# A ring of split projection weights placed 64 bytes lower in a one-core hybrid decoder block

## The chip, the cores and the metric

The kernel runs on one NeuronCore of one Trainium2 chip. The metric is the device time of one execution in microseconds (us); a lower time is better. The clock of TensorE (PE in the profile) has two levels in these records, 1.2 and 2.4 GHz, and the profile gives the granted share of the upper one.

## What is computed

One decoder layer on 16 meta tokens and 512 real tokens, width 2048: an RMS norm, one wide input projection, a gated DeltaNet branch, a pooling branch, a gated merge with an output projection, and a SwiGLU feed-forward part. Cut to what matters here:

```python
h = concatenate([meta, x], axis=1)                 # 528 tokens
hn = rms_norm(h, norm_mix_w)
proj = hn @ w_in                                   # q, k, v, z, beta/decay logits, p, gate_a, gate_b
q, k, v = silu(causal_dwconv(qkv)); q, k l2-normed
o = gated_delta_rule_chunked(q, k, v, beta, g)     # 8 heads of 128
y_a = (rms(o) * silu(z)) @ w_proj_a
y_b = (pool(p) @ pool_w * pool_scale) @ w_proj_b
h += (sigmoid(gate_a) * y_a + sigmoid(gate_b) * y_b) @ w_out
h += (silu(rms_norm(h) @ w_gate) * (rms_norm(h) @ w_up)) @ w_down
out = rms_norm(h)[:, 16:]
```

All products keep close to float32: both operands are split into a high part (rounded to fp32r) and a low part (the remainder), and three products are summed: high by high, high by low, low by high.

## The kernel before, in words

**Stages, in order of time.** The weights `w_in` are read in chunks of 128x1024 floats (512 KB); four chunks make a unit of 256 output channels, and a chunk holds four of the 16 blocks of 128 input channels (`kt = c + 4*k` for chunk `c` of the unit and `k` from 0 to 3). Each chunk lands in `w_raw` by a DMA of SP, ScalarE (ACT) rounds it into `w_hi` (line 935), VectorE (DVE) subtracts and writes `w_lo` (line 1378), and TensorE multiplies. `w_raw`, `w_hi` and `w_lo` have four slots each; chunk `c` of every unit uses slot `c`.

- First unit (`first_unit`, line 2105): one unit of q/k/v; all its products with tokens 0 to 255 (moving operand 256 wide), then all with tokens 256 to 527 (272 wide).
- Stage A (line 2128, `chunk_products`): 11 more units of q/k/v. The moving operand comes from `hn_halves`: for each stationary block a product 256 wide and one 272 wide, so 11 x 4 x 2 x 4 x 3 = 1056 such pairs.
- Stage G (2128 again): 16 units for the gates, interleaved with the DeltaNet recurrence's small matmuls; the moving operand is `hn_real`, all 512 real tokens at once: 16 x 96 = 1536 matmuls.
- Stage P: 4 units for the pooling input, `hn_halves`: 384 pairs.
- Stage Z: 4 units for z, `hn_real`: 384 matmuls of 512.
- Merge (2128, tiles `w_hi_m`, `w_lo_m`), then the output projection (2432 to 2434), the feed-forward gate and up products (2457 to 2459, 44 units of 7 x 24 = 168 matmuls 256 wide) and the down projection (2432 to 2434 again, 512 wide).

The order of TensorE's work is written out by hand and the same before and after. Before a chunk TensorE waits for `lo_ready` (the count of DVE's low parts); ACT waits for `chunk_used` before it writes a slot again.

**Where the tiles lie.** What the change touches is addresses. All begin as offsets in bytes within a partition, and the code asserts that `whi_at`, `wlo_at`, `mixer_consts_at`, `hn_at` and `ext_at` are the same modulo `BEAT` = 256; call that place 0. Worked out from there:

- `w_hi` slot `c` begins at 64 + 4160*c from `whi_at`. As 4160 = 16*256 + 64, its place modulo 256 is 64*(c+1). A stationary block inside begins at a multiple of 512 further on, so it has the place of its slot. `w_lo` is laid out alike. `w_hi_m` and `w_lo_m` (merge) have no gaps: place 0.
- `hn_hi[:, kt, :]` and `hn_lo[:, kt, :]` have rows of 528 floats = 2112 = 8*256 + 64 bytes. With `kt = c + 4*k`, row `kt` has place 64*c. `hn_halves` begins at its column 0 or 256: place 64*c. `hn_real` begins at column 16, 64 bytes on: place 64*(c+1).
- Merge and down projection: both operands at place 0.
- Feed-forward: the moving tiles `s_hi`, `s_lo` are at `hn_at + 64`, place 64; the stationary tiles `hi_a`, `lo_a`, `hi_b`, `lo_b`, `hi_c`, `lo_c` at place 0. One stationary pair differs from unit to unit: `hi_2_0`, `lo_2_0` (place 0) serve units 4 to 43, `hi_2_1`, `lo_2_1` (place 64) serve units 0 to 3; the program's names for both in the trace are `hi` and `lo`, used in the third product (S2) of each unit.

```python
def two(tiles, n):
    return tiles[1] if isinstance(n, int) and n < STEADY else tiles[0]
```

Of the kernel before, what the change touches and what calls it, by code (L numbers as in the profile page):

```python
# [140 lines left out]
def hybrid_block(nc, x, meta_tokens, norm_mix_w, w_in, conv_w, a_log, dt_bias, o_norm_w, w_proj_a, pool_w,  # L141
                 pool_scale, w_proj_b, w_out, norm_ffn_w, w_ffn_gate, w_ffn_up, w_ffn_down, norm_final_w, out):
    ctx = ExitStack()
    with ctx:
# [14 lines left out]
        def place(name, shape, dtype=F32, at=None):  # L159
            size = int(np.prod(shape[1:])) * 4  # L160
            offset = top[0] if at is None else at
            if at is None:
                top[0] += (size + 63) // 64 * 64
            return nc.alloc_sbuf_tensor_at(name, shape, dtype, offset=offset)
# [5 lines left out]
        def ring(name, step, first):  # L170
            return [place(f"{name}{i}", [P, CHUNK], F32R, at=top[0] + first + (4 * CHUNK + step) * i) for i in range(SLOTS)]

        LINE = 64
        whi_at = top[0]
        whi, whi_m = ring("w_hi", LINE, LINE), ring("w_hi_m", 0, 0)
        top[0] += SLOTS * (4 * CHUNK + LINE)
        wlo_at = top[0]
        wlo, wlo_m = ring("w_lo", LINE, LINE), ring("w_lo_m", 0, 0)
        top[0] += SLOTS * (4 * CHUNK + LINE)

        minus_half = place("minus_half", [P, 16])
# [2335 lines left out]
```

## Time and profile before

| | |
|---|---|
| median of 3 runs | 2654.39 us (2654.24 to 2655.65) |
| the profiled execution | 2655.96 us, its span 2654.2 us |
| mean granted TensorE clock | 0.993 |
| busy: PE, PE weight load, DVE, ACT, POOL | 98%, 89%, 68%, 38%, 12% |
| HBM | 151 GB/s mean over the span |

The profile shows one execution. A matmul's duration in it is from its start to the end of its results, and successive matmuls overlap; what a matmul costs in a stream is the distance from its start to the next one's. The timeline view prints starts to 0.01 us and merges neighbours that use the same tiles into one row ("x2").

### The profile page before, as it was taken

How to read it: one execution, taken by the hardware profiler on the slowest of the kernel's cores; microseconds unless marked ns; L12 is line 12 of the kernel's file. 1: busy time of each engine (PE TensorE's matmuls, PEld its weight loads, DVE VectorE, ACT ScalarE, POOL GpSimd, SP SyncE). 2: the span in 40 equal slices, each digit the busy share in tenths (PEclk: the TensorE clock that was granted, in tenths of full speed). 3: DMA queues.
4: the chain of work that ended last, by engine and by line, in shares of the span. 5: the costliest groups of instructions: out<-in, count | busy, mean ns of one | idle time of the engine just before them, and what ended most of it. 6: DMA issues, size and time to landing. Idle time of an engine off the chain costs nothing.

```text
span 2654.2 us, 43654 instructions
## 1 busy us (share of the span) xinstructions
PE 2604.5 (98%) x17278; PEld 2369.4 (89%) x17278; DVE 1816.0 (68%) x1714; ACT 999.0 (38%) x1016; POOL 318.9 (12%) x326
## 2 busy tenths in 40 slices
PE   7999999999999999999989999999999999999998
PEld 6999988888889977888879999999999998888886
DVE  5444555554543234558888888888888888888898
ACT  4443322222222232223454444444444444333334
POOL 6000034444431500100000000000000000000000
PEclk8999999999999999999999999999999999999999
DMA  4333333333333434689333444544454449866562
GB/s 145 98 87 95 84 87 88 91 83 91 88 90 92 110 87 165 231 282 324 127 138 124 161 155 148 173 153 156 147 179 150 154 150 344 279 198 218 161 203 102
DMA packets 346856, 400.84 MB, mean 151 GB/s; under 512 B 11626, under 2 KB 300563, under 8 KB 345619
## 3 DMA queue, kind: packets, MB, share of 16 engines
q1 hardware_dynamic: 287122, 335.39, 40.4%
q10 hardware_dynamic: 59664, 64.51, 7.1%
q8 instruction: 46, 0.75, 0.1%
q14 instruction: 24, 0.19, 0.0%
HBM read 328.02 MB, written 71.84 MB: 151 GB/s over the span
## 4 chain that ended last, share of the span: by engine, by line
PE 92%; DVE 3%; issue 1%; ACT 1%; DMA 1%; POOL 1%; SPq 0%; DVEq 0%; ACTq 0%; POOLq 0%
PE psum L2128 34%; PE psum L2457 10%; PE psum L2459 10%; PE psum L2458 10%; PE psum L2432 7%; PE psum L2433 6%; PE psum L2434 6%; PE psum L2286 2%; PE psum L2105 1%; PE psum L2297 1%; DMA w_raw<-in_w_proj_a 1%; PE psum L2372 1%; PE psum L2267 0%; DMA dn_raw<-in_w_ffn_down 0%; POOL hn_lo L766 0%
## 5 line engine op out<-in xcount | busy, mean ns | idle before, releaser
L2128 PE MATMUL psum<-hn_hi,w_hi 128*128 128x256 f32 (+1 forms) x1600 | 451.2, 331 | 0.0
L2128 PE MATMUL psum<-hn_lo,w_hi 128*128 128x256 f32 (+1 forms) x1600 | 450.0, 330 | 0.0
L2128 PE MATMUL psum<-hn_hi,w_lo 128*128 128x256 f32 (+1 forms) x1600 | 449.3, 330 | 0.0
L1378 DVE TENSOR_TENSOR w_lo<-w_raw,w_hi 128x1024 fp32r<-128x1024 f32 x144 | 190.1, 1321 | 260.7 <-ACT w_hi L935 259.7
L935 ACT ACTIVATE w_hi<-w_raw 128x1024 fp32r<-128x1024 f32 x144 | 152.2, 1058 | 415.8 <-PE psum L2128 387.6
L2128 PEld LDWEIGHTS psum<-hn_hi,w_hi 128*128 128x128 f32 x1600 | 271.0, 188 | 22.8 <-issue 0.2
L2128 PEld LDWEIGHTS psum<-hn_lo,w_hi 128*128 128x128 f32 x1600 | 270.8, 188 | 22.9 <-issue 0.7
L2128 PEld LDWEIGHTS psum<-hn_hi,w_lo 128*128 128x128 f32 x1600 | 270.5, 188 | 22.7
L2432 PE MATMUL psum<-dn_hi,act_hl 128*128 128x512 f32 x616 | 240.9, 391 | 2.0 <-DVE dn_lo L1712 2.0
L2434 PE MATMUL psum<-dn_hi,act_hl 128*128 128x512 f32 x616 | 240.3, 390 | 0.0
L2433 PE MATMUL psum<-dn_lo,act_hl 128*128 128x512 f32 x616 | 240.2, 390 | 0.0
L2457 PE MATMUL psum<-s_hi,hi_a 128*128 128x256 f32 x704 | 194.6, 276 | 1.0 <-DVE s_lo L1883 1.0
L2458 PE MATMUL psum<-s_lo,hi_a 128*128 128x256 f32 x704 | 194.4, 276 | 0.0
L2459 PE MATMUL psum<-s_hi,lo_a 128*128 128x256 f32 x704 | 194.4, 276 | 0.0
L2459 PE MATMUL psum<-s_hi,lo_b 128*128 128x256 f32 x704 | 194.4, 276 | 0.0
L2458 PE MATMUL psum<-s_lo,hi_c 128*128 128x256 f32 x704 | 194.4, 276 | 0.0
L2459 PE MATMUL psum<-s_hi,lo_c 128*128 128x256 f32 x704 | 194.4, 276 | 0.0
L2458 PE MATMUL psum<-s_lo,hi_b 128*128 128x256 f32 x704 | 194.4, 276 | 0.0
L2457 PE MATMUL psum<-s_hi,hi_c 128*128 128x256 f32 x704 | 194.4, 276 | 0.0
L2457 PE MATMUL psum<-s_hi,hi_b 128*128 128x256 f32 x704 | 194.4, 276 | 0.0
L920 POOL TENSOR_TENSOR rms<-rms_a,minus_half 128x1 f32<-128x1 f32 x4 | 2.6, 658 | 1281.9 <-DVE rms_a L2025 1281.9
L1185 ACT ACTIVATE hi<-t 128x1024 fp32r<-128x1024 f32 x44 | 46.8, 1064 | 267.9 <-DVE t L1829 267.9
(359 smaller groups left out, 6236.0 us busy)
## 6 DMA issues: line engine op xcount, KB each, us to landing
w_raw<-in_w_in SPq DMA_DIRECT2D x144, 512.0 KB, 3.9
ffn_raw<-in_w_ffn_gate SPq DMA_DIRECT2D x44, 1024.0 KB, 6.4
ffn_raw<-in_w_ffn_up SPq DMA_DIRECT2D x44, 1024.0 KB, 6.9
dn_raw<-in_w_ffn_down SPq DMA_DIRECT2D x32, 1024.0 KB, 8.3
act_hl<-act_dram SPq DMA_DIRECT2D x56, 512.0 KB, 9.1
act_dram<-comb_hi ACTq DMA_DIRECT2D x22, 896.0 KB, 4.2
act_dram<-comb_lo ACTq DMA_DIRECT2D x22, 896.0 KB, 6.2
out_raw<-in_w_out SPq DMA_DIRECT2D x16, 1024.0 KB, 10.9
```

The source lines that it names most:

```text
L935: act.activation(whi[s][:], raw[s][:], ACT.Copy).then_inc(S["hi_ready"], 1)
L1185: act.activation(two(hi_2s, n)[:], two(t2s, n)[:], ACT.Copy).then_inc(S["hi_ready"], 1)
L1378: dve.tensor_tensor(wlo[s][:], raw[s][:], whi[s][:].bitcast(F32), ALU.subtract).then_inc(S["lo_ready"], 1)
L2105: ins = pe.matmul(outs(m)[i], lhs, mv, start=kt == 0 and j == 0, stop=kt == KT - 1 and j == 2)
L2128: ins = pe.matmul(o, lhs, r, start=kt == 0 and i == 0, stop=kt == 4 * n_chunks - 1 and i == 2)
L2286: ins = pe.matmul(bank(1)[:, i, :], x[:, i, :], B[11][:, i, :], start=True, stop=True)
L2432: pe.matmul(out, a_hi, w_hi, start=start and i == 0, stop=False, skip_group_check=True)
L2433: pe.matmul(out, a_hi, w_lo, start=False, stop=False, skip_group_check=True)
L2434: ins = pe.matmul(out, a_lo, w_hi, start=False, skip_group_check=True, stop=i == k - 1 and (what in ("b21", "b22", "t4") or at_end and wha ...
L2457: pe.matmul(out, w_hi[:, k0 + k, :], s_hi[c][:, k, :], start=start and k == 0, stop=False, skip_group_check=True)
L2458: pe.matmul(out, w_hi[:, k0 + k, :], s_lo[c][:, k, :], start=False, stop=False, skip_group_check=True)
L2459: ins = pe.matmul(out, w_lo[:, k0 + k, :], s_hi[c][:, k, :], start=False, stop=stop and k == HEADS - 1, skip_group_check=True)
```

## The change

The two rings of the projection's weights lose their first 64 bytes; the distance between slots stays 4160, and `top` moves on by as much as before, so no other tile moves. The merge's tiles (`w_hi_m`, `w_lo_m`) stay.

```diff
         LINE = 64
         whi_at = top[0]
-        whi, whi_m = ring("w_hi", LINE, LINE), ring("w_hi_m", 0, 0)
+        whi, whi_m = ring("w_hi", LINE, 0), ring("w_hi_m", 0, 0)
         top[0] += SLOTS * (4 * CHUNK + LINE)
         wlo_at = top[0]
-        wlo, wlo_m = ring("w_lo", LINE, LINE), ring("w_lo_m", 0, 0)
+        wlo, wlo_m = ring("w_lo", LINE, 0), ring("w_lo_m", 0, 0)
         top[0] += SLOTS * (4 * CHUNK + LINE)
```

with

```python
def ring(name, step, first):
    return [place(f"{name}{i}", [P, CHUNK], F32R, at=top[0] + first + (4 * CHUNK + step) * i) for i in range(SLOTS)]
```

Slot `c` then has place 64*c. No instruction is added, removed or moved on any engine.

## Rows read from the trace of the kernel before

**Rows 1.** The page: the span, busy time and share of each engine.

```profile
span 2654.2 us, 43654 instructions
...
PE 2604.5 (98%) x17278; PEld 2369.4 (89%) x17278; DVE 1816.0 (68%) x1714; ACT 999.0 (38%) x1016; POOL 318.9 (12%) x326
```

**Rows 2.** The page: the chain that ended last, by engine.

```profile
PE 92%; DVE 3%; issue 1%; ACT 1%; DMA 1%; POOL 1%; SPq 0%; DVEq 0%; ACTq 0%; POOLq 0%
```

**Rows 3.** The view of waits, for PE: who it waited for, us, times, longest.

```profile
PE psum L2457 <- DVE s_lo L1907: 7.9, 1, 7.9
PE psum L2105 <- DVE w_lo L1378: 5.3, 3, 3.0
...
PE psum L2128 <- DVE gate_a L1769: 1.0, 1, 1.0
```

**Rows 4.** The groups by form: line 2128's matmuls, one of each width.

```profile
L2128 PE MATMUL psum<-hn_hi,w_hi 128*128 128x512 f32 x640 | 256.8, 401 | 0.0
...
L2128 PE MATMUL psum<-hn_hi,w_lo 128*128 128x272 f32 x480 | 138.4, 288 | 0.0
...
L2128 PE MATMUL psum<-hn_lo,w_hi 128*128 128x256 f32 x480 | 134.4, 280 | 0.0
```

**Rows 5.** Timeline of PE, stage A; each x2 is one pair.

```profile
266.59 0.40 PE L2128 MATMUL psum<-hn_hi,w_hi 128*128 128x256 f32 x2
266.83 0.40 PE L2128 MATMUL psum<-hn_lo,w_hi 128*128 128x256 f32 x2
...
268.03 0.40 PE L2128 MATMUL psum<-hn_hi,w_hi 128*128 128x256 f32 x2
```

**Rows 6.** Timeline of PE, feed-forward unit 3: S2 begins and ends.

```profile
1440.73 0.28 PE L2459 MATMUL psum<-s_hi,lo_a 128*128 128x256 f32 x1
...
1441.86 0.28 PE L2457 MATMUL psum<-s_hi,hi 128*128 128x256 f32 x1
...
1444.74 0.28 PE L2457 MATMUL psum<-s_hi,hi_b 128*128 128x256 f32 x1
```

**Rows 7.** Timeline of PE, unit 4: S2 begins and ends.

```profile
1461.06 0.28 PE L2457 MATMUL psum<-s_hi,hi 128*128 128x256 f32 x1
...
1463.78 0.28 PE L2457 MATMUL psum<-s_hi,hi_b 128*128 128x256 f32 x1
```

**Rows 8.** Timeline of PE, first unit, 256 wide alone: chunk 1's second half, chunk 3.

```profile
35.55 0.28 PE L2105 MATMUL psum<-hn_hi,w_hi 128*128 128x256 f32 x1
...
36.85 0.28 PE L2105 MATMUL psum<-hn_hi,w_lo 128*128 128x256 f32 x1
...
44.59 0.28 PE L2105 MATMUL psum<-hn_hi,w_hi 128*128 128x256 f32 x1
...
47.21 0.28 PE L2105 MATMUL psum<-hn_hi,w_lo 128*128 128x256 f32 x1
```

**Rows 9.** Timeline of PE, first unit, 272 wide alone: chunk 0 and chunk 1's start.

```profile
55.03 0.29 PE L2105 MATMUL psum<-hn_hi,w_hi 128*128 128x272 f32 x1
...
57.99 0.29 PE L2105 MATMUL psum<-hn_hi,w_hi 128*128 128x272 f32 x1
```

**Rows 10.** Timeline of PE, merge, 512 wide.

```profile
1119.96 0.39 PE L2128 MATMUL psum<-zb_hi,w_lo_m 128*128 128x512 f32 x1
...
1122.91 0.39 PE L2128 MATMUL psum<-zb_hi,w_hi_m 128*128 128x512 f32 x1
```

**Rows 11.** Timeline of PE, stage Z: first matmuls of two successive chunks, 24 apart.

```profile
921.58 0.39 PE L2128 MATMUL psum<-hn_hi,w_hi 128*128 128x512 f32 x1
...
927.06 0.39 PE L2128 MATMUL psum<-hn_hi,w_hi 128*128 128x512 f32 x1
```

**Rows 12.** Timeline of PE, feed-forward units 1 and 2: product A12 and S2.

```profile
1400.01 0.28 PE L2457 MATMUL psum<-s_hi,hi_a 128*128 128x256 f32 x1
...
1402.83 0.28 PE L2457 MATMUL psum<-s_hi,hi 128*128 128x256 f32 x1
...
1422.67 0.28 PE L2457 MATMUL psum<-s_hi,hi 128*128 128x256 f32 x1
```

**Rows 13.** The lines of the two splits: ns min/median/max, first and last start.

```profile
L1378 DVE TENSOR_TENSOR w_lo<-w_raw,w_hi x144: 1209/1225/2065, 25.5 to 985.5; 128x1024 fp32r<-128x1024 f32 x144
L1378 DVE TENSOR_TENSOR w_lo_m<-w_raw,w_hi_m x32: 1214/1225/1229, 1002.4 to 1178.7; 128x1024 fp32r<-128x1024 f32 x32
...
L935 ACT ACTIVATE w_hi<-w_raw x144: 1038/1059/1066, 23.7 to 984.4; 128x1024 fp32r<-128x1024 f32 x144
L935 ACT ACTIVATE w_hi_m<-w_raw x32: 1039/1047/1062, 1001.3 to 1177.6; 128x1024 fp32r<-128x1024 f32 x32
```

## The prediction

> **What bounds the kernel now.** I read the page first: PE is busy for 98% of the span [rows 1], and the chain that ended last runs over PE for 92% [rows 2]. The waits say the same from the other side: the longest single waits of PE are 7.9 and 5.3 us, and in the stages that use the rings (line 2128) it waited 1.0 us for one producer [rows 3]. So whatever changes the distance between two matmul starts in those stages lands in the time one for one, and nothing else in the change can. The change adds no instruction; it moves the stationary operand of line 2128 and line 2105 by 64 bytes against the moving one. What has to be priced is therefore a distance in ns, times a count. The counts are in the groups by form [rows 4]: three groups of 480 pairs (256 and 272 wide) make 1440 pairs in stages A and P, and three of 640 make 1920 matmuls 512 wide in stages G and Z.
>
> **What the spacing is now, and at which offset.** I call offset the place of the moving operand less that of the stationary one, modulo 256 bytes.
>
> - Stages A and P have offset -64. Six pairs start in 268.03 - 266.59 = 1.44 us, so a pair costs 240.0 ns [rows 5].
> - Merge has offset 0: 13 matmuls of 512 in 2.95 us, 226.9 ns each [rows 10]. I take this as the undisturbed rate. Scaled by width it is 113.5 ns for 256 columns and 120.6 for 272. The feed-forward part shows 113.3 for 256, below.
> - The feed-forward part has offset +64: in unit 4, 24 matmuls take 1463.78 - 1461.06 = 2.72 us, 113.3 ns each [rows 7].
>
> At the undisturbed rate a pair would take 113.3 + 120.4 = 233.7 ns (272/256 of 113.3 is 120.4), so today's pairs cost 6.3 ns more than that.
>
> **The row that speaks of alignment.** The kernel itself holds one trial of offset 0 at width 256. S2 of units 0 to 3 reads its stationary tile at place 64, where the moving tile is too; from unit 4 on the same product reads it at place 0. In unit 3, S2's 24 matmuls take 1444.74 - 1441.86 = 2.88 us, 120.0 ns each [rows 6], and the ten matmuls just ahead of it, at offset +64, took 1.13 us, 113 ns each [rows 6]. In unit 4 S2 has 113.3 ns [rows 7]. Nothing else differs between these places but 64 bytes of the stationary tile's address. So equal places cost 6.7 ns per matmul at width 256, and the address does matter. At width 512 equal places cost nothing in merge [rows 10]: a weight load of 128 columns has twice the time there, and I take it that this is why.
>
> The Trainium skill (TensorE: Matmul & The Clock Gate, step 1 of "What happens when you issue a matmul") says the opposite of the unit-3 row: PE has two independent SBUF read ports, so that loading the next weights doesn't take bandwidth from the running matmul. By that rule the move would change nothing, and 120.0 against 113.3 ns should not be there.
>
> **The change part by part.**
>
> 1. Stages A and P go from offset -64 to 0, 1440 pairs. For the 256-wide half the nearest row is S2 of unit 3: 120.0 ns. For the 272-wide half no row shows offset 0. Lower end: 120.4, its undisturbed rate, if the 16 further columns give the weight load the room it lacks; upper end: 120.4 + 6.7 = 127.1. Between them I take 123.5: in the first unit 272-wide matmuls run back to back and 24 of them take 57.99 - 55.03 = 2.96 us, 123.5 ns [rows 9]; that excess comes with the odd width, which the change doesn't touch. Sum: 243.5 ns for a pair, 3.5 ns more than now, x1440 = **+5.0 us**. The bounds of a pair are 240.4 (+0.6 us) and 247.1 (+10.2 us) if the S2 row carries over; and 233.7 (-9.1 us) if it does not.
> 2. First unit, offset -64 to 0. Alone, the 256-wide matmuls stand at 1.30 us for 11, 118 ns, in chunk 1, and at 2.62 us for 23, 114 ns, in chunk 3 [rows 8]. To 120.0 from between these is +4 ns on the some 60 that run at the full clock: **+0.3 us**. The second pass, 96 matmuls, stays as taken above; at most +3.6 ns x 96 = +0.3.
> 3. Stages G and Z go from offset 0 to +64, 1920 matmuls. A chunk in stage Z takes 927.06 - 921.58 = 5.48 us for 24, 228.3 ns [rows 11], against 226.9 undisturbed. Lower end: nothing is disturbed, -1.4 ns x 1920 = -2.7 us. Upper end: offset +64 isn't always clean; in unit 1 A12 takes 1402.83 - 1400.01 = 2.82 us for 24, 117.5 ns [rows 12], which is 4.2 over 113.3. Laid on the undisturbed 512-wide matmul that makes 231.1, +2.8 on today's 228.3, x1920 = +5.4 us. I take the middle, **+1.0 us** (rounded down, since the width gives room).
> 4. ACT's and DVE's splits write and read at moved addresses. Their medians in the ring's tiles are 1059 and 1225 ns, in the merge's tiles at place 0 1047 and 1225 ns [rows 13]: at most 12 ns in a thousand, and both engines have hundreds of us to spare there, so **0**. The cover is that PE is behind, not they: it waited for `w_lo` only in the first unit [rows 3].
> 5. The DMAs write `w_raw`, which doesn't move: **0**.
>
> Sum: +5.0 + 0.3 + 1.0 = **+6.3 us**. Against the profiled execution (2655.96 us, its span 2654.2 and 1.8 around it) that is 2662.3; that execution was 1.6 us above the median, so on the median of 2654.39 it is **2660.7 us**. A measurement of this kernel tells 0.2%, 5.3 us, from no change; the forecast lies just beyond.
>
> **The rivals.**
>
> - *Equal places are what the projection wants.* The 6.3 ns excess of today's pair would be the price of offset -64 and would go: 1440 x -6.3 = -9.1 us, with the first unit -9.3, with G and Z between -2.7 and +5.4: about **2645.5 us**. For it: merge runs at offset 0 without any excess [rows 10], and stage Z, offset 0, is nearly clean [rows 11]. Against: both are 512 wide; the only 256-wide row at offset 0 is a slow one [rows 6], and 256-wide matmuls at offset -64 reached 114 ns in chunk 3 of the first unit [rows 8], so -64 alone isn't the cause.
> - *Nothing that can be measured.* Either the pair's excess belongs to the width of 272 and the weight load finds its room (240.4, +0.9 with the first unit), with G and Z near zero, or the offset plays no part in this stage and the pair stays at 240.0; or A and P lose what G and Z gain. **2654 to 2657 us**. (The middle one of these is what the Trainium skill's rule above would give.) That the change doesn't do what it says in half of its places belongs here: only `hn_halves` comes to lie equal; `hn_real`, equal before, is 64 bytes off afterwards.
> - *The feed-forward part stays in its slower rhythm.* Units 1 and 2 run at 117.5 ns, the rest at 113.3, with the same tiles and offsets; the step down came at S2 of unit 2, from 1422.67 on [rows 12]. A rhythm that outlasts its cause can hang on when a wait falls, and the change shifts everything before it. Decisive is whether the rhythm changes by unit 3, the last with S2 at equal places. If not, 168 x 4.2 ns = 0.7 us for each of 41 units, **+29 us: 2683 us** without the rest. Against: the rhythm is set after waits of DVE in unit 0 [rows 3], which the projection doesn't touch.
>
> **How the numbers follow.** The forecast's case, dearer pairs (240.4 up to 247.1 with G and Z on their dear side), has 0.43; the slow rhythm 0.03. The faster rival has 0.26. No measurable difference has 0.28, which includes forecasts of +1 to +5 us. Slower over 0.2% is then 0.46, within 0.28, faster 0.26. The range goes from the faster rival, 2645, to the upper bound of the pair with G and Z a little dearer: 2654.4 + 10.2 + 0.3 + about 3 = 2668. It leaves out the slow rhythm, the dearest G and Z together with the dearest pairs, and a faster case in which A, P, G and Z all gain. The likeliest case's own range is 2656 to 2668.
>
> **What would show it.** Right: in stage A six pairs take 1.46 us (243.5 ns each) instead of 1.44; stage Z's chunks take 5.45 to 5.55 us; feed-forward, merge and down projection keep every spacing; PE still waits for nothing at line 2128. Wrong in step 1: six pairs in 1.40 us (the faster rival) or 1.44 (no difference). Wrong in step 3: a chunk in stage Z outside 5.44 to 5.55 us. The slow rhythm would show as 2.82 us for S1 of unit 4 instead of 2.72. A difference that sits in ACT, DVE or DMA waits ahead of line 2128 would make the whole reading wrong.

## The result, and the profile after

The changed kernel takes 2662.61 us (median of 9 runs, 2661.89 to 2664.45) against 2655.65 us (9 runs) of the kernel before beside it: 7.0 us more, a ratio of 1.0028 with a 95% interval of 1.0018 to 1.0038. The difference is clear of noise and small, under 0.3%. The forecast was +6.3 us.

The page of the kernel after, span and busy time:

```profile
span 2660.4 us, 43654 instructions
...
PE 2608.3 (98%) x17278; PEld 2371.5 (89%) x17278; DVE 1816.7 (68%) x1714; ACT 999.2 (38%) x1016; POOL 318.7 (12%) x326
```

Against [rows 1] the span is 6.2 us longer with the same instructions; PE's busy time rose by 3.8 us and that of its weight loads by 2.1; DVE, ACT and POOL stay within 0.7. The view of waits for PE is as in [rows 3], with 1.6 us more in the first unit, over three waits whose longest is 3.0 us as before:

```profile
PE psum L2457 <- DVE s_lo L1907: 7.9, 1, 7.9
PE psum L2105 <- DVE w_lo L1378: 6.9, 3, 3.0
```

Stage A begins only 0.42 us later all the same, so these waits cannot be the 6.2 us; the time is in the spacing. The timeline of PE gives the start of each stage. Before, the first matmul of stages A, G, P, Z and of merge:

```profile
68.20 0.39 PE L2128 MATMUL psum<-hn_hi,w_hi 128*128 128x256 f32 x1
...
328.39 0.39 PE L2128 MATMUL psum<-hn_hi,w_hi 128*128 128x512 f32 x1
...
823.73 0.37 PE L2128 MATMUL psum<-hn_hi,w_hi 128*128 128x256 f32 x1
...
916.10 0.40 PE L2128 MATMUL psum<-hn_hi,w_hi 128*128 128x512 f32 x1
...
1018.05 0.49 PE L2128 MATMUL psum<-o_hi,w_hi_m 128*128 128x512 f32 x1 [0.37 <-DVE win L1668]
```

and after:

```profile
68.62 0.51 PE L2128 MATMUL psum<-hn_hi,w_hi 128*128 128x256 f32 x2
...
332.28 0.39 PE L2128 MATMUL psum<-hn_hi,w_hi 128*128 128x512 f32 x1
...
828.55 0.36 PE L2128 MATMUL psum<-hn_hi,w_hi 128*128 128x256 f32 x1
...
922.22 0.39 PE L2128 MATMUL psum<-hn_hi,w_hi 128*128 128x512 f32 x1
...
1024.60 0.50 PE L2128 MATMUL psum<-o_hi,w_hi_m 128*128 128x512 f32 x1 [0.34 <-issue]
```

The differences of neighbouring rows: up to stage A +0.42 us, then A 260.19 to 263.66 (+3.47), G 495.34 to 496.27 (+0.93), P 92.37 to 93.67 (+1.30), Z up to merge 101.95 to 102.38 (+0.43). That is +6.55, and what comes behind gives some 0.4 back. A and P make three quarters of the change.

The +0.42 up to stage A is only in part the change's. The first unit's second pass, from its first to its last matmul, takes 11.74 us before and 11.96 after; 11.74 and 11.96 come back in every kernel below whose second pass has the offset and widths of the one or the other, so +0.22 us is the change's. The rest lies in the first pass, which waits for DVE and runs in part at the lower clock (starts 0.21 us apart instead of 0.12, as from 41.09 us on before): in the profiled executions of seven kernels with the first unit of before (before itself among them), stage A begins anywhere from 66.57 to 69.40 us.

The timeline of PE after, stage A, which answers to [rows 5]:

```profile
265.40 0.41 PE L2128 MATMUL psum<-hn_hi,w_hi 128*128 128x256 f32 x2
265.64 0.41 PE L2128 MATMUL psum<-hn_lo,w_hi 128*128 128x256 f32 x2
...
266.86 0.41 PE L2128 MATMUL psum<-hn_hi,w_hi 128*128 128x256 f32 x2
```

Six pairs take 1.46 us, 243.3 ns each, where they took 1.44. Two successive chunks of stage Z, which answer to [rows 11], now begin

```profile
927.73 0.40 PE L2128 MATMUL psum<-hn_hi,w_hi 128*128 128x512 f32 x1
...
933.24 0.39 PE L2128 MATMUL psum<-hn_hi,w_hi 128*128 128x512 f32 x1
```

5.51 us apart, 229.6 ns for a matmul where it was 228.3. Last, the feed-forward part after: S2's first matmul in unit 1, two neighbours of the product behind it (S1), and S2's first matmul in unit 2.

```profile
1409.32 0.28 PE L2457 MATMUL psum<-s_hi,hi 128*128 128x256 f32 x1
...
1414.57 0.28 PE L2457 MATMUL psum<-s_hi,hi_b 128*128 128x256 f32 x1
1414.68 0.28 PE L2458 MATMUL psum<-s_lo,hi_b 128*128 128x256 f32 x1
...
1428.51 0.28 PE L2457 MATMUL psum<-s_hi,hi 128*128 128x256 f32 x1
```

Neighbours are 0.11 us apart already in unit 1, and S2 of unit 2 comes 19.19 us after S2 of unit 1, where before it took 1422.67 - 1402.83 = 19.84 us [rows 12]. The slower rhythm ended one unit earlier, and that gave 0.65 us back.

### The profile page after: what moved, and what is told of

It reads as the page before. It is cut to its first block, busy times and chain, and to the rows that moved or that the text cites. A ratio compares the mean times of both kernels' runs of the same rounds, so it can differ in the third digit from the quotient of the medians.

```text
span 2660.4 us, 43654 instructions
## 1 busy us (share of the span) xinstructions
PE 2608.3 (98%) x17278; PEld 2371.5 (89%) x17278; DVE 1816.7 (68%) x1714; ACT 999.2 (38%) x1016; POOL 318.7 (12%) x326
## 4 chain that ended last, share of the span: by engine, by line
PE 92%; DVE 3%; issue 1%; DMA 1%; ACT 1%; SPq 1%; POOL 1%; DVEq 0%; ACTq 0%; POOLq 0%
PE psum L2128 35%; PE psum L2457 10%; PE psum L2459 10%; PE psum L2458 10%; PE psum L2432 6%; PE psum L2433 6%; PE psum L2434 6%; PE psum L2286 2%; PE psum L2105 1%; PE psum L2297 1%; DMA dn_raw<-in_w_ffn_down 1%; DMA w_raw<-in_w_proj_a 1%; PE psum L2372 1%; PE psum L2267 0%; DVE out_lo L1712 0%
## 5 line engine op out<-in xcount | busy, mean ns | idle before, releaser
L2432 PE MATMUL psum<-dn_hi,act_hl 128*128 128x512 f32 x616 | 240.8, 391 | 2.2 <-DVE dn_lo L1712 1.8
```

The lines of the kernel that those rows point to most:

```text
L2432: pe.matmul(out, a_hi, w_hi, start=start and i == 0, stop=False, skip_group_check=True)
```

## The experiments

Theory 1: the spacing is set by the offset of the moving against the stationary operand, modulo 256 bytes. Rivals: the ring's own place counts, or where the splits write; only equal places are dear; the width of 272 makes the excess. All stage times below are, as above, differences of the first matmuls' starts in the timeline of one profiled execution of each kernel. Stages that a kernel leaves alone agree between kernels to some 0.05 us unless the text says otherwise, which is what makes differences of 0.4 us readable. Z takes 101.95 us before.

| kernel | offset in A, P | in G, Z | A | G | P | ratio to before, 95% |
|---|---|---|---|---|---|---|
| before | -64 | 0 | 260.2 | 495.3 | 92.4 | |
| after | 0 | +64 | 263.7 | 496.3 | 93.7 | 1.0028 (1.0018 to 1.0038) |
| A alone | A 0, P -64 | 0 | 263.7 | 495.3 | 92.4 | 1.0015 (1.0005 to 1.0025) |
| all but A | A -64, P 0 | +64 | 260.2 | 496.3 | 93.7 | 1.0012 (1.0003 to 1.0022) |
| both 64 lower | -64 | 0 | 260.2 | 495.7 | 92.4 | 1.0000 (0.9990 to 1.0009) |
| ring at 192 | +64 | 128 | 266.1 | 498.6 | 93.5 | 1.0113 (with a wait, below) |
| ring at 128 | 128 | -64 | 266.3 | 499.2 | 94.7 | one run |

**One part of the change alone.** A second pair of tile names on the same memory lets the stages differ; the last unit of A already splits into the other ring (`wlo_a` is made alike, and the products of the first unit and of stage A read both).

```diff
         whi, whi_m = ring("w_hi", LINE, LINE), ring("w_hi_m", 0, 0)
+        whi_a = ring("w_hi_a", LINE, 0)
...
-                    split(G_A + 4 * u + c + 4, c)
+                    split(G_A + 4 * u + c + 4, c, *((whi, wlo) if isinstance(u, int) and u == N_A - 1 else (whi_a, wlo_a)))
```

> The change's placement (first byte at 0) for the first unit and stage A alone; stages G, P and Z keep the ring of before (64). Theory 1, the spacing of the matmuls is set by the offset between moving and stationary operand: stage A takes 263.7 us as with the whole change (before 260.2), stages G, P, Z take 495.3, 92.4 and 102.0 us as before; in all +3.7 us (first unit 0.2, A 3.5), less up to 0.9 us if the feed-forward part changes its rhythm one unit earlier as with the change, so 2658 to 2659.5. Rival, the cost comes from where the splits write against everything else, or from the change as a whole shifting waits: A's gain or loss would not stand alone and G, P, Z would move too.

Measured: 2659.25 us against 2656.17. The stages begin at

```profile
67.03 0.39 PE L2130 MATMUL psum<-hn_hi,w_hi_a 128*128 128x256 f32 x1
...
330.68 0.40 PE L2130 MATMUL psum<-hn_hi,w_hi 128*128 128x512 f32 x1
...
826.01 0.37 PE L2130 MATMUL psum<-hn_hi,w_hi 128*128 128x256 f32 x1
```

so A takes 263.65 us, G 495.33: all of A's loss and nothing of G's. The complement swaps the two rings' places.

> The complement of the run with stage A alone: first unit and stage A keep the ring at 64, stages G, P and Z get the change's 0. Theory 1 (each stage pays for its own offset): A 260.2, G 496.3, P 93.7, Z 102.4, that is +0.9 +1.3 +0.4 = +2.7 us in these stages, the whole 2657 to 2658.5. Rival (what one stage pays depends on the one before): G or Z off these by over 0.3 us.

Measured: 2659.01 us against 2655.53, +3.5, and 0.5 us above the expected 2657 to 2658.5; the profiled stages fit:

```profile
69.00 0.39 PE L2130 MATMUL psum<-hn_hi,w_hi_a 128*128 128x256 f32 x1
...
329.20 0.39 PE L2130 MATMUL psum<-hn_hi,w_hi 128*128 128x512 f32 x1
...
825.54 0.36 PE L2130 MATMUL psum<-hn_hi,w_hi 128*128 128x256 f32 x1
```

A 260.20, G 496.34, and P 93.7, Z 102.4. Stage A begins at 69.00 us here instead of 68.20, with the first unit of before: that is the scatter of the first pass named above, and of the size of the miss. Each stage pays for its own offset, and the two parts add up to the whole (+3.1 and +3.5 against +7.0).

**Relative or absolute.** Two small tiles ahead of the tokens are packed, so that `hn_hi` and `hn_lo` too lie 64 bytes lower:

```diff
-        whi, whi_m = ring("w_hi", LINE, LINE), ring("w_hi_m", 0, 0)
+        whi, whi_m = ring("w_hi", LINE, 0), ring("w_hi_m", 0, 0)
...
-        g_all = place("g_all", [P, CH + 1, HEADS])
-        b_all = place("b_all", [P, CH + 1, HEADS])
+        g_all = place("g_all", [P, CH + 1, HEADS], at=top[0])
+        b_all = place("b_all", [P, CH + 1, HEADS], at=top[0] + 160)
+        top[0] += 320
...
+        top[0] += LINE
+        hn_at = top[0] - 2 * KT * TOK * 4
```

> The change, and with it the token tiles hn_hi and hn_lo also 64 bytes lower (two small tiles ahead of them packed to make room, the recurrent state with them). Ring and tokens stand to each other as before the change (A and P at -64, G and Z at 0), while both stand 64 bytes lower against everything else. Theory 1 (relative offset): stage A 260.2 us, G 495.3, P 92.4, Z 102.0, a pair 240.0 ns, the time that of before within 2 us. Rival (the place of the ring itself, against w_raw or against the splits' writes): A 263.7, G 496.3, P 93.7, Z 102.4 as with the change, +6.

Measured: 2655.6 us, the ratio 1.0000. Stage A runs from

```profile
68.27 0.39 PE L2129 MATMUL psum<-hn_hi,w_hi 128*128 128x256 f32 x1
...
328.44 0.39 PE L2129 MATMUL psum<-hn_hi,w_hi 128*128 128x512 f32 x1
```

in 260.17 us with the ring exactly where the change puts it. The rival of the ring's own place, against `w_raw` or the splits' writes, falls; the loss is one of the relation between ring and tokens. G is 0.4 us over that of before, where five other kernels with G at offset 0 lie within 0.05 us of it and one (the halves apart by 24, below) is 0.7 over; the recurrent state moved too in this kernel, and I leave that open.

**The other two offsets.** `first` is 192 or 128 instead of 64; 16 unused columns of `small` (and, for 192, the space of `ssq`) make room, and the merge's first split waits for the last z chunk, because the rings' tails now reach into `w_lo_m`.

```diff
-        whi, whi_m = ring("w_hi", LINE, LINE), ring("w_hi_m", 0, 0)
+        whi, whi_m = ring("w_hi", LINE, 192), ring("w_hi_m", 0, 0)
...
-                        act.wait_ge(S["chunk_used"], g - (SLOTS - 1))
+                        act.wait_ge(S["chunk_used"], g - (SLOTS - 1) + 3 * (g == G_MERGE))
```

> Both rings begin 192 bytes up instead of 64, so stages A and P run at offset +64 (modulo 256: moving less stationary, 0 - 192) and G and Z at -128. For room the 16 unused columns of two small tiles are given up, and the merge's first split waits until the last z chunk is used (some 2 to 6 us in merge, on the path, not part of the theory). Theory 1 (offset decides): A and P behave as the feed-forward part does at +64, 113.3 to 117.6 ns for 256 wide; a pair 234 to 238 ns instead of 240.0, stage A 254 to 258 us. Rival theory 2, only equal places are dear and all other offsets are alike: pair 240.0, A 260.2. Rival theory 3, the width of 272 alone makes the excess: 240 too. G and Z are open: 227 to 231 ns.

> Both rings begin 128 bytes up, so stages A and P run at offset 128 and G and Z at -64. The same room is made and the same extra wait stands at merge's first split. Theory 1: another pair cost than at 0 (243.3) and -64 (240.0), with no row to say which; between 234 and 244. Theory 2 (only equal places are dear): 240.0. Z at -64: between 226.7 and 229.5 ns.

Measured: 2685.51 us and, in one run, 2688.76 us, some 29 and 33 us over before. More than half of it is that wait, which I had priced at 2 to 6 us; the timeline of the kernel with 192 has it at

```profile
1046.68 0.79 PE L2128 MATMUL psum<-o_hi,w_hi_m 128*128 128x512 f32 x1 [16.70 <-DVE win L1668]
```

The stages ahead of it are clean of it. Stage A with the ring at 192, and with 128:

```profile
68.58 0.39 PE L2128 MATMUL psum<-hn_hi,w_hi 128*128 128x256 f32 x1
...
334.70 0.39 PE L2128 MATMUL psum<-hn_hi,w_hi 128*128 128x512 f32 x1
```

```profile
68.67 0.38 PE L2128 MATMUL psum<-hn_hi,w_hi 128*128 128x256 f32 x1
...
335.00 0.39 PE L2128 MATMUL psum<-hn_hi,w_hi 128*128 128x512 f32 x1
```

266.1 and 266.3 us. My number for +64 (254 to 258, taken from the feed-forward part) is wrong by 8 us, and "only equal places are dear" is wrong too: in stage A the pairs are cheapest at -64, then 0, then +64 and 128.

In stage P the order is not the same: 92.4 at -64, then 93.5 at +64, 93.7 at 0 and 94.7 at 128. The pairs at +64 have two prices. Instructions, widths and offsets are those of stage A, where a chunk of 24 pairs takes 5.91 to 5.92 us (246.5 ns a pair), but in P two chunks of the kernel with 192 begin at

```profile
862.60 0.28 PE L2128 MATMUL psum<-hn_hi,w_hi 128*128 128x256 f32 x1
...
868.43 0.28 PE L2128 MATMUL psum<-hn_hi,w_hi 128*128 128x256 f32 x1
```

5.83 us apart, 243 ns a pair. At -64, 0 and 128 a chunk takes the same in A as in P (5.77, 5.85 and 5.92 us). So at +64 something besides the offset chooses between two rhythms, and these runs do not show what. In G and Z the order is another: 0, then +64, then 128, then -64, by the sums of G in the table and by a chunk of Z (5.48, 5.51, 5.58 and 5.60 us). So the offset counts, but which one is good depends on the widths that follow one another, and at +64 on the rhythm too; a rate measured at one width does not carry over. The ring of before was at the best of the four places for both kinds of stage.

**Half of the change.** Only `w_hi` moves.

```diff
-        whi, whi_m = ring("w_hi", LINE, LINE), ring("w_hi_m", 0, 0)
+        whi, whi_m = ring("w_hi", LINE, 0), ring("w_hi_m", 0, 0)
```

> Half of the change: w_hi begins at 0, w_lo stays at 64. Two of three products take w_hi. If each weight load costs by its own offset alone, two thirds of the change: A 262.5, P 93.2, G 496.0. If the stream's rhythm is what counts, in which a load at another place upsets its neighbours, more than that: A 263.7 or above.

Measured in one run: 2664.26 us; A 262.8, P 93.3 and G 497.2 us. A has 76% of the whole change's loss and P 73%, a little over the two thirds of single loads. G is worse than with the whole change (496.3), and so is Z (102.75 against 102.38), which no sum over single loads gives. In G and Z a matmul's price is not independent of its neighbours.

**Another cut of the tokens**, at 272 instead of 256, on both rings.

```diff
-EARLY = 256
+EARLY = 272
```

> The kernel before with the tokens cut at 272 instead of 256, so that the 272-wide half comes first and the 256-wide half begins 64 bytes on modulo 256. Ring at 64: the wide half is at offset -64, the narrow half at 0. If the excess of 6.3 ns of a pair hangs on the width, 240.0 stays and A is 260.2. By theory 1 with S2's row (256 wide at offset 0: 120.0) a pair costs 120.0 + 123.5 = 243.5, A 263.9, P 93.7, in all +5 us. If the contiguous order of the reads helps, A 254 to 258 and the kernel beats both.

> The same cut at 272 with the rings of the change (0): the wide half is at offset 0, the narrow half at +64, where the feed-forward part runs at 113.3 or 117.6 ns. By widths and offsets taken one by one: 113.3 to 117.6 + 120.4 to 127.1, a pair 234 to 245 ns, A 254 to 265. If the pair as a whole sets it and its first half decides, as the change: 243.3, A 263.7. G and Z as with the change, 496.3 and 102.4.

Measured: 2662.72 us (ratio 1.0027, 1.0016 to 1.0037) with A 265.9 us, and 2664.55 us (one run) with A 266.3. Both miss my numbers on the high side. G and Z are untouched (495.4 and 496.3, 101.9 and 102.5), as they must be. The same widths in the other order cost 5.7 us more in A alone: neither the width of 272 nor the offset of each half by itself sets the price of a pair. Nor does the order by itself. In the first of these kernels chunks 1, 2 and 3 of stage A begin at

```profile
74.23 0.29 PE L2128 MATMUL psum<-hn_hi,w_hi 128*128 128x272 f32 x1
...
80.01 0.29 PE L2128 MATMUL psum<-hn_hi,w_hi 128*128 128x272 f32 x1
...
85.92 0.29 PE L2128 MATMUL psum<-hn_hi,w_hi 128*128 128x272 f32 x1
```

The first of them takes 5.78 us, 240.8 ns a pair, close to the kernel before; the next takes 5.91, and all later ones 5.92, 246.7 ns. P does the same, with 5.76 and 5.77 us ahead of 5.91. The stream starts in a rhythm near that of before and slips into a slower one with the same instructions; what makes it slip is not shown.

**The halves apart.** If the sequence counts, alternating widths is a choice. Stages with two moving halves take a branch of their own, in which the loop over the halves (`p`) stands outside those over the products, first over 12 products, then over a whole chunk of 24. The branch for 12:

```diff
                 pe.wait_ge(S["lo_ready"], g + 1)
+                if len(outs(0)) == 2:
+                    for m in range(2):
...
+                        for n, (p, k, i) in enumerate((p, k, i) for p in range(2) for k in range(4) for i in range(3)):
...
+                            ins = pe.matmul(outs(m)[p], lhs, mv[p], start=kt == 0 and i == 0, stop=kt == KT - 1 and i == 2)
...
+                    return
```

> The kernel before (ring at 64) with the two token halves of stages A and P taken apart: for each 128 output channels of a chunk first the 12 products 256 wide, then the 12 that are 272 wide, instead of alternating. Offset -64 throughout. Theory 1 with the first unit's rows: 256 wide alone runs at 113.3 ns or in the slower rhythm at 117.6, 272 wide alone at 123.5; that makes 236.8 to 241.1 for both against 240.0 now, A 256.8 to 261.3 us, the whole 2651 to 2657. Rival: every change of width upsets the rhythm for about ten matmuls, as a change of chunk does in stage Z, and A rises above 262.

> As the one before it, but apart over a whole chunk: 24 products 256 wide, then 24 that are 272 wide, as in the first unit. Fewer changes of width: if these upset the rhythm, this one is faster than the other by that. Theory 1: 236.8 to 241.1 ns for both halves, A 256.8 to 261.3 us, the whole 2651 to 2657 us; below 2650 would beat both kernels measurably.

Measured: 2654.53 us for 12 (ratio 0.9995, 0.9986 to 1.0004; A 259.3), 2667.35 us for 24 (1.0042, 1.0028 to 1.0056; A 267.8). The second is slower for another reason, which its view of waits for PE shows:

```profile
PE psum L2128 <- ACT conv_in L974: 7.9, 10, 0.9
```

Both halves of both PSUM groups end late in a unit and are needed at once in the next. The last spacing of each unit is 1.06 us in its stage A, ten times over; without these, A would be some 258.4 us. So 24 was kept for chunks 1 and 2 of a unit, and 12 for chunks 0 and 3.

> The token halves taken apart over a whole chunk in chunks 1 and 2 of each unit, and by 12 in chunks 0 and 3, where the banks change hands. If the waits of the version with 24 everywhere come from the banks alone, they are gone: no first spacing of 223 ns in a unit, A 257.5 to 259.3 us, P 91.5 to 92.1, the whole 2652 to 2655 us. If changes of order inside a unit upset the rhythm, A 260 or above.

Measured: 2651.94 us against 2655.53, a ratio of 0.9988 (0.9979 to 0.9997), A 258.2 and P 91.6 us. That is 3.6 us under the kernel before, by little, and the interval only just leaves out no difference; A and P have 2.7 of it in the profiled execution. The kernel after was not run beside it; 2651.94 is far under its 2662.61. The long spacings between units are gone, as they should be if the banks alone made them. A chunk of 24 and 24 in its timeline:

```profile
189.74 0.28 PE L2128 MATMUL psum<-hn_hi,w_hi 128*128 128x256 f32 x1
...
192.47 0.28 PE L2128 MATMUL psum<-hn_hi,w_hi 128*128 128x272 f32 x1
...
195.43 0.28 PE L2128 MATMUL psum<-hn_hi,w_hi 128*128 128x256 f32 x1
```

2.73 us for 24 of 256 (113.8 ns) and 2.96 for 24 of 272 (123.3 ns): at offset -64 the narrow ones all but reach 113.3 ns, and the wide ones do not reach 120.4. A pair's worth is 237.1 ns.

**The rhythm of the feed-forward part.** S2 of units 0 to 3 reads the tile at place 0. `two` also picks where these tiles are written, so the writes move along.

```diff
-    return tiles[1] if isinstance(n, int) and n < STEADY else tiles[0]
+    return tiles[0]
```

> The kernel before, with S2 of feed-forward units 0 to 3 reading its stationary tile at place 0 as all later units do. Theory 1: S2 of units 1 to 3 falls from 120.0 ns to what the products around it have, 113.3 or 117.6. Theory on the rhythm: the step from 117.6 to 113.3 ns came from S2 at equal places; without it the 117.6 rhythm goes on, +29 us, some 2684 us. Rival: the step comes from a small wait in unit 2 (one start 115 ns after the one before), whatever S2 reads; then the rest runs at 113.3 and the kernel is 0.5 us faster or the same.

Measured: 2686.39 us against 2656.17, a ratio of 1.0116 (1.0099 to 1.0133), +30 us. Its timeline, S2 of unit 4:

```profile
1461.91 0.28 PE L2457 MATMUL psum<-s_hi,hi 128*128 128x256 f32 x1
...
1464.74 0.28 PE L2457 MATMUL psum<-s_hi,hi_b 128*128 128x256 f32 x1
```

24 matmuls in 2.83 us, 117.9 ns, with the tiles, offsets and widths of [rows 7], where they take 113.3. Units 4 to 43 take 791.5 us instead of 761.6, so the slower rhythm lasts for all of them. Taking the equal places away removes the step down: a product that is slower (120.0 ns) than its neighbours is needed to put the stream into the faster rhythm. All 13 other kernels kept the equal places and made the step at S2, of unit 1 or of unit 2: the product ahead of it runs at 117.7 to 117.8 ns, the one behind it at 113.3.

Equal places do not suffice, and the kernel before shows it. Its S2 of unit 1 begins at 1402.83 [rows 12] and the product behind it at

```profile
1405.71 0.28 PE L2457 MATMUL psum<-s_hi,hi_b 128*128 128x256 f32 x1
```

2.88 us for 24, 120.0 ns, at equal places; yet S2 of unit 2 comes 16.96 us or 144 matmuls later [rows 12], 117.8 ns each. The step waits for that next S2. The small wait that I had named as a rival (a start 115 ns after the one before) is not what makes it either: it is there in most of the kernels at the S2 that makes the step, but with the halves apart by 12 that S2 starts after 117 ns and the step comes all the same. What lets one S2 make the step and another not stays open.

## Why the prediction was right

- **What bounds the kernel**: right. The loss is in PE's spacing; the waits at line 2128 for `gate_a` went from 1.0 to 1.2 us. Two readings of the waits were wrong, and nothing rests on them: 5.3 us is the sum of three waits, the longest 3.0 us, and the longest single wait of the kernel before is another,

```profile
PE psum L2144 <- DMA rows_b<-in_o_norm_w: 8.2, 1, 8.2
```

 the same after.
- **Step 1, pairs from -64 to 0, +5.0 us, 243.5 ns**: measured 243.3 ns and 3.47 + 1.30 = +4.8 us. The size is right; its make-up is only half right. In the first unit after the change, where widths stand alone, the 256-wide matmuls do have S2's rate,

```profile
46.09 0.28 PE L2105 MATMUL psum<-hn_hi,w_hi 128*128 128x256 f32 x1
...
47.53 0.28 PE L2170 MATMUL psum<-hn_hi,ab_hl 128*32 128x256 f32 x1
```

 12 in 1.44 us, 120.0 ns, but the 272-wide ones do not stay at 123.5:

```profile
58.25 0.29 PE L2105 MATMUL psum<-hn_hi,w_hi 128*128 128x272 f32 x1
...
61.26 0.30 PE L2105 MATMUL psum<-hn_hi,w_hi 128*128 128x272 f32 x1
```

 24 in 3.01 us, 125.4 ns. The sum of the two alone would be 245.4; alternating they cost 2.1 ns less. Two errors of mine, the wide half taken as untouched and the halves taken as additive, cancelled: that the sum came out within 0.2 ns was luck. The thought that 16 further columns might give the weight load room did not come true either, and that its double time is why 512-wide matmuls bear equal places was not tested. The runs with the cut at 272 show that adding rates by width is not a method to rely on.
- **Step 2, first unit, +0.3**: +0.42 up to stage A in the profiled executions. The second pass, 272 wide, has +0.22 of it, within the nothing to 0.3 that I gave it; the first pass scatters by more than the rest, so the +0.3 put on it is neither borne out nor refuted as a time.
- **Step 3, G and Z, +1.0, a chunk of Z in 5.45 to 5.55 us**: 5.51 us, +0.93 + 0.43 = +1.4 us. Right in sign and size. The reason given for the upper end, the slow rhythm of the feed-forward part, was not what came; Z's matmuls run at 229.6, not 231.1. G lost less than Z, 0.6 ns a matmul against 1.1.
- **Steps 4 and 5, nothing in ACT, DVE and DMA**: right; the kernel with ring and tokens both 64 lower has the splits' new addresses and no loss.
- **"Feed-forward keeps every spacing"**: wrong by 0.65 us. The step to the faster rhythm came in unit 1 instead of 2. As kernels with either placement show it in unit 1 (and the ring at 128 and 192 in unit 2), it is not tied to the change.
- **The faster rival** (equal places are what the projection wants) fell: offset -64 is the cheapest of the four for pairs. **The rival of no difference** fell too: 64 bytes of placement move stage A by 3.5 us. The Trainium skill (TensorE: Matmul & The Clock Gate, step 1 of "What happens when you issue a matmul") has loading the next weights take no read bandwidth from the running matmul; what I drew from that, that the move would change nothing, the runs do not bear out, and where in the chip the two meet they do not show. **The slow rhythm** did not come, but its price, forecast as +29 us, was measured as +30 when it was brought about; the step is what it hangs on, and it failed to come only where S2's place was changed.

## What to carry to other kernels

Where TensorE streams without waits, read starts, not busy time: a spacing above the width's best rate, constant over hundreds of matmuls, can be a cost of placement, of the sequence of widths, or of a slower rhythm. The first 64 bytes moved a stage here by 0.2 to 1.4%. Try the few relative places for each sequence of widths rather than carrying a rate over from another stage, and don't tidy an odd offset away because equal places look right. A product that looks slow by itself may be what changes the rhythm of everything behind it, so measure its removal on the whole.

## What the runs showed of the hardware that I had not expected

- The time between matmuls depends on the offset between moving and stationary operand; of the four places 64 bytes apart that were tried, stage A takes 260.2, 263.7, 266.1 and 266.3 us at -64, 0, +64 and 128. Moving both operands 64 bytes lower together leaves stage A at 260.2.
- The dependence differs with the widths in the stream: 512-wide ones are best at 0 (228.3 ns in stage Z, 229.6 at +64), alternating 256 and 272 at -64. The other order of the two widths cost 5.7 us in stage A, once its stream had slipped into the slower rhythm.
- A stream has more than one lasting rhythm for the same instructions: 113.3 or 117.8 ns at width 256, held for 40 units, 761.6 or 791.5 us, to their end. Alternating pairs have it too: 243 or 246.5 ns at offset +64, and with the wide half first 240.8 ns at the start and 246.7 later.
- What in the chip makes the dependence on placement and the two rhythms is not shown by these runs and stays open. That places count modulo 256 bytes fits what is seen: from one `k` of a chunk to the next the moving operand moves by 8448 bytes and the stationary one by 1024, so their distance changes by 29 x 256, and in stage A before every pair still takes 240 ns; 64 and 128 bytes do make a difference.
